# Second-mixer weights split into two parts once, kept in HBM, and loaded as two parts by every group

## What is computed

```python
# layer 0, token mixer A: gated MLP with a masked 128x128 mixing matrix per channel group
u, v, z = split(h @ w_in, 3)                       # a_w_in: 1024 x 6144
y = gelu(u) * (mix(layer_norm(gelu(v))) + b_s) * silu(z)
x = x + gate_a * (y @ w_out)                       # a_w_out: 2048 x 1024
# once: the shared keys and values
k, v = split(rms_norm(x, kv_norm) @ w_kv, 2)       # w_kv: 1024 x 256, rotary on k
# layer 1, token mixer B: sliding-window attention with sinks
q, z = split(h @ b_w_in, 2)                        # b_w_in: 1024 x 2048, rotary on q
o = softmax_with_sink(q k^T in bands of 128) @ v
x = x + gate_b * ((o * silu(z)) @ b_w_out)         # b_w_out: 1024 x 1024
return rms_norm(x, final_norm)
```

## Time and profile before

| | us |
|---|---|
| median of 3 runs | 2426.22 |
| lowest and highest of them | 2418.42 and 2426.76 |
| the profiled execution, its own time | 2430.8 |
| its span on the core | 2429.0 |
| PE busy in the span | 2274.2 |
| DVE, POOL, ACT busy | 1314.8, 1116.1, 947.8 |

### The profile page before, as it was taken

The page is one execution under the profiler, slowest core; times in us unless marked ns, Lnnn a source line. Parts: engine busy times, 40 slices in busy tenths (PEclk is TensorE's granted clock), DMA queues, the critical chain, the costliest instruction groups (busy, mean ns, idle before and its releaser), DMA issues.

```text
span 2429.0 us, 28242 instructions
## 1 busy us (share of the span) xinstructions
PE 2274.2 (94%) x10725; PEld 1899.4 (78%) x10725; DVE 1314.8 (54%) x1767; ACT 947.8 (39%) x1730; POOL 1116.1 (46%) x646
## 2 busy tenths in 40 slices
PE   3999999999999999999999999969789989998898
PEld 2787878888888888888888888857767877787786
DVE  5647891315744315644414554266577577657854
ACT  3223233433333433333423333344445545445553
POOL 3345554444444344444444443424544555564554
PEclk9999999999999999999999999989899999999999
DMA  7753334433434333344333346473634464573433
GB/s 278 268 202 114 128 130 165 165 97 120 147 113 169 128 119 117 121 144 156 121 104 105 122 140 224 134 251 102 237 106 159 176 239 132 187 256 130 156 113 113
DMA packets 188327, 375.73 MB, mean 155 GB/s; under 512 B 14272, under 2 KB 85024, under 8 KB 187552
## 3 DMA queue, kind: packets, MB, share of 16 engines
q1 hardware_dynamic: 185760, 368.65, 44.3%
q10 hardware_dynamic: 2432, 5.28, 0.6%
HBM read 295.23 MB, written 69.21 MB: 150 GB/s over the span
## 4 chain that ended last, share of the span: by engine, by line
PE 76%; DVE 10%; DMA 5%; DVEq 2%; issue 2%; ACT 2%; POOL 1%; SPq 1%; POOLq 0%; ACTq 0%
PE ps L1461 23%; PE ps L1463 23%; PE ps L1462 23%; PE ps L1611 2%; DMA w_raw<-in_a_w_out 1%; DMA r<-b_input 1%; PE ps L1649 1%; PE ps L1650 1%; POOL w_lo L704 1%; DVE wh L1305 1%; DVEq L1404 1%; DVE y_hl L1259 1%; DVE qs L1375 1%; DMA w_raw<-in_b_w_in 1%; PE ps L1673 1%
## 5 line engine op out<-in xcount | busy, mean ns | idle before, releaser
L704 POOL TENSOR_TENSOR w_lo<-w_raw,w_hi 128x1024 fp32r<-128x1024 f32 x360 | 900.9, 2513 | 991.1 <-ACT w_hi L814 990.7
L814 ACT ACTIVATE w_hi<-w_raw 128x1024 fp32r<-128x1024 f32 x360 | 380.3, 1061 | 822.6 <-DMA w_raw<-in_a_w_in 519.0
L1461 PE MATMUL ps<-h,w_hi 128*128 128x512 f32 x1024 | 402.3, 393 | 0.0
L1462 PE MATMUL ps<-h,w_hi 128*128 128x512 f32 x1024 | 398.9, 390 | 0.0
L1463 PE MATMUL ps<-h,w_lo 128*128 128x512 f32 x1024 | 398.8, 389 | 0.0
L1461 PE MATMUL ps<-r,w_hi 128*128 128x512 f32 x512 | 212.9, 416 | 26.8 <-DMA r<-b_input 11.3
L1463 PEld LDWEIGHTS ps<-h,w_lo 128*128 128x128 f32 x1024 | 192.5, 188 | 40.6
L1462 PEld LDWEIGHTS ps<-h,w_hi 128*128 128x128 f32 x1024 | 192.6, 188 | 39.5 <-issue 0.2
L1461 PEld LDWEIGHTS ps<-h,w_hi 128*128 128x128 f32 x1024 | 192.6, 188 | 39.2 <-POOL w_lo L704 0.2
L1462 PE MATMUL ps<-r,w_hi 128*128 128x512 f32 x512 | 206.1, 403 | 0.0
L1463 PE MATMUL ps<-r,w_lo 128*128 128x512 f32 x512 | 206.1, 402 | 0.0
(11 more groups left out here) (200 smaller groups left out, 4093.1 us busy)
## 6 DMA issues: line engine op xcount, KB each, us to landing
w_raw<-in_a_w_in SPq DMA_DIRECT2D x256, 256.0 KB, 3.0
w_raw<-in_a_w_in SPq DMA_DIRECT2D x64, 512.0 KB, 4.7
w_raw<-in_a_w_out SPq DMA_DIRECT2D x64, 512.0 KB, 4.1
w_raw<-in_b_w_in SPq DMA_DIRECT2D x64, 512.0 KB, 4.6
kv_input<-xks SPq DMA_DIRECT2D x32, 512.0 KB, 5.7
b_input<-hbs SPq DMA_DIRECT2D x32, 512.0 KB, 6.5
r<-b_input SPq DMA_DIRECT2D x16, 1024.0 KB, 10.9
w_raw<-b_out_gated SPq DMA_DIRECT2D x32, 512.0 KB, 4.2
```

What stands on the lines that cost most here:

```text
L704: g.tensor_tensor(wlo[p][:, rows_], raw[p][:, rows_], whi[p][:, rows_].bitcast(F32), ALU.subtract).then_inc(w_lo, 1)
L814: s_.activation(whi[p][:, rows_], raw[p][:, rows_], ACT.Copy).then_inc(w_hi, 1)
L1461: t_.matmul(dst_, stat[0], mov[0], start=start, stop=False)
L1462: t_.matmul(dst_, stat[0], mov[1], start=False, stop=False)
```

## The change

The weights of the second mixer are split once. The 26 halves (`SPLIT_UNITS`: kv, then q, z and b) are taken one for each stage of the first mixer (`LOAD_STAGES`: six in group 0, nine in each of groups 1 and 2, two in group 3). A stage is one slab j of v or one channel group g. In stage q SP loads a half into `wsr`; in stage q + 1 ACT rounds it into `wsh`, POOL subtracts into `wsl` (and multiplies by the gate first for b); in stage q + 2 SP stores both parts to `wsd` in HBM. In the second mixer each half is then loaded as two transfers, straight into `w_hi` and `w_lo`, and PE waits on the transfers. ACT's `hi` and POOL's `lo` are gone there, and so is the separate gating of b_w_out. The core of the diff:

```diff
+SPLIT_UNITS = [("kv", 0, 0)] + [(kind, n, ku) for kind in "qzb" for n in range(2) for ku in range(2)]
+SPLITS = 2 * len(SPLIT_UNITS)
+LOAD_STAGES = [(i, q) for i in range(NG) for q in range(1 if i else 4, 10)][:SPLITS]
...
+def split_at(i, q, later):
+
+    return LOAD_STAGES.index((i, q - later)) if (i, q - later) in LOAD_STAGES else None
...
-            return 16 * sum(2 if w < FIRST_B and U_UZ <= w % A_UNITS < U_AO else 1 for w in range(u % 2, u + 1, 2))
+
+            return 16 * sum(2 if w >= FIRST_B or U_UZ <= w % A_UNITS < U_AO else 1 for w in range(u % 2, u + 1, 2))
...
             def b_half(u, hh):
                 p = u % 2
-                kind, g, n, ku = B_UNITS[u - FIRST_B]
-                there = raw[p][:, 2 * hh:2 * hh + 2]
+                for m, w in ((0, whi[p]), (1, wlo[p])):
+                    sp.dma_start(w[:, 2 * hh:2 * hh + 2].bitcast(F32), wsd[split_of(u, hh), m]) \
+                        .then_inc(raw_in[2 * p + hh], 16)
+
+            def load_split(s):
+                m, (kind, n, ku), hh = s % 2, SPLIT_UNITS[s // 2], s % 2
                 kt = 4 * ku + 2 * hh
+                if s >= 2:
...
+            def keep_split(s):
+                sp.wait_ge(split_lo, s + 1)
+                sp.dma_start(wsd[s, 0], wsh[s % 2][:].bitcast(F32)).then_inc(split_out[s % 2], 16)
+                sp.dma_start(wsd[s, 1], wsl[s % 2][:].bitcast(F32)).then_inc(split_out[s % 2], 16)
+
+            def split_stage(i, q):
+                for later, act_ in ((2, keep_split), (0, load_split)):
+                    s = split_at(i, q, later)
+                    if s is not None:
+                        act_(s)
...
-                    for n in range(2):
-                        sp.wait_ge(wb_out[n], 16 * KT // 2)
+                    split_stage(i, j)
...
                         keep_turned(i - 1, g - 2)
-                    if i == 1 and g == 2:
+                    if g < GROUPS:
+                        split_stage(i, 4 + g)
...
+            def split(i, q):
+
+                s = split_at(i, q, 1)
+                if s is None:
+                    return
+                m, (kind, n, ku) = s % 2, SPLIT_UNITS[s // 2]
+                if kind == "b":
+                    pool.wait_ge(dve_pro, 4)
+                    pool.wait_ge(split_in[m], 16 * (s // 2 + 1))
+                    pool.nop(nofuse=True)
+                    g.tensor_tensor(wsr[m][:], wsr[m][:], gate_b[:, None, 512 * n:512 * n + 512].broadcast_to([P, 2, T]),
+                                    ALU.mult).then_inc(split_gated, 1)
+                pool.wait_ge(split_hi, s + 1)
+                g.tensor_tensor(wsl[m][:], wsr[m][:], wsh[m][:].bitcast(F32), ALU.subtract).then_inc(split_lo, 1)
...
                 for n in range(3, 10):
                     lo(first + n)
+                    if n % 2 == 1:
+                        split(i, (n - 3) // 2)
...
-                for u, hh in weights_at(pc):
-                    lo(u, (hh,))
...
+            def split(i, q):
+
+                s = split_at(i, q, 1)
+                if s is None:
+                    return
+                m = s % 2
+                if SPLIT_UNITS[s // 2][0] == "b":
+                    act.wait_ge(split_gated, s + 1 - 2 * SPLIT_UNITS.index(("b", 0, 0)))
+                else:
+                    act.wait_ge(split_in[m], 16 * (s // 2 + 1))
+                if s >= 2:
+                    act.wait_ge(split_out[m], 32 * (s // 2))
+                s_.activation(wsh[m][:], wsr[m][:], ACT.Copy).then_inc(split_hi, 1)
...
                     hi(first + U_UZ + 2 * g + 3)
+                    split(i, 4 + g)
...
-                for u, hh in weights_at(pc):
-                    hi(u, (hh,))
...
                 p = u % 2
                 if kt % 4 == 0:
-                    pe.wait_ge(w_lo, 2 * u + kt // 4 + 1)
+                    pe.wait_ge(raw_in[2 * p + kt // 4], landed(u))
```

More of the change, by code:

```diff
@@ L121, in order, with splits_by, split_of @@
     return (k % 4, k // 4) if by_halves(u) else (k // 2, k % 2)
[L124 to L134, removed]
+SPLIT_UNITS = [("kv", 0, 0)] + [(kind, n, ku) for kind in "qzb" for n in range(2) for ku in range(2)]
[3 more added lines that the diff above has]
+    return LOAD_STAGES.index((i, q - later)) if (i, q - later) in LOAD_STAGES else None
+def splits_by(i, m):
+    return sum(1 for s, (g, _) in enumerate(LOAD_STAGES) if g <= i and s % 2 == m)
+def split_of(u, hh):
+    kind, g, n, ku = B_UNITS[u - FIRST_B]
+    return 2 * SPLIT_UNITS.index((kind, n, ku)) + hh
 def turned_at(pc):
@@ L257, in yoco_kernel @@
         zo = [place(f"zo{n}", gb_at + 2 * K * n, [T], F32) for n in range(2)]
-        fn = place("fn", region(4 * K), [D], F32)
-        cs = place("cs", region(4 * K), [2, T], F32)
+        fn_at, cs_at = region(4 * K), region(4 * K)
+        fn = place("fn", fn_at, [D], F32)
+        cs = place("cs", cs_at, [2, T], F32)
         hfx_at, xst_at = region(4 * K), region(4 * K)
@@ L335, in yoco_kernel @@
         xr_in, xl_in = sem("xr_in", 16), sem("xl_in")
-        wb_in, wb_out = [sem(f"wb_in{n}") for n in range(2)], [sem(f"wb_out{n}") for n in range(2)]
+        split_in, split_out = [sem(f"split_in{n}") for n in range(2)], [sem(f"split_out{n}") for n in range(2)]
         sw_in = [sem(f"sw_in{n}") for n in range(2)]
@@ L359, in yoco_kernel @@
         sin_done = sem("sin_done")
-        w_lo = sem("w_lo")
+        w_lo, split_lo = sem("w_lo"), sem("split_lo")
         pool_pro, pool_mask, zeroed = sem("pool_pro"), sem("pool_mask"), sem("zeroed")
         x_rstd, v_rstd, x1_rstd, x2_rstd = sem("x_rstd", 1), sem("v_rstd", 1), sem("x1_rstd", 1), sem("x2_rstd", 4)
-        p_norm, pt_masked, wb_gated = sem("p_norm"), sem("pt_masked"), sem("wb_gated")
+        p_norm, pt_masked, split_gated = sem("p_norm"), sem("pt_masked"), sem("split_gated")
         dve_pro, ada_used = sem("dve_pro"), sem("ada_used")
@@ L439, in _ @@
             wb = b_w_in[0].rearrange("(k p) n -> p k n", p=P)
-            wbo = wbod.rearrange("k p n -> p k n")
+            wbo = b_w_out[0].rearrange("(k p) n -> p k n", p=P)
             def a_half(u, hh):
@@ L760, in _ @@
                     g.memset(kvf[:, 0, P:2 * P], 0.0).then_inc(zeroed, 1)
-                lo(first + 32)
-                lo(first + 33)
+                else:
+                    lo(first + 32)
+                    lo(first + 33)
             x1_stage(NG - 1)
@@ L849, in turned_round @@
                 act.wait_ge(t1_full, at("t1_full", i, kt + 1))
-                if i == 0 and kt == 0:
-                    act.wait_ge(wb_out[0], 16 * KT // 2)
                 if before:
@@ L884, in _ @@
                     hi(first + 2 * j + 3)
+                    split(i, j)
                 if i == 0:
@@ L1739, in b_piece @@
                 if k in ((0, 4) if by_halves(u) else (0, 1)):
-                    pe.wait_ge(w_lo, 2 * u + hh + 1)
+                    pe.wait_ge(raw_in[2 * (u % 2) + hh], landed(u))
                 if k == 0 and kind == "b":
```

49 lines of the change are left out of this document (17 added, 32 removed).

## The result

The changed kernel takes 2477.4 us (median of four runs, 2474.8 to 2481.1), the kernel before, run beside it, 2424.6: a ratio of 1.022, 95% interval 1.020 to 1.025. That is 53 us slower, and slower than the range of the prediction. In the one profiled execution that each trace shows, the difference is smaller, 2474.9 - 2429.0 = 45.9 us of span: that of the kernel before was one of its slower ones.

The account below looks back on a forecast made before the run. PE was taken to bound the first mixer, and late softmax work and transfers to idle it in the second. 34.5 + 22.6 - 36 = +21 us on 2430.8 gave 2451.9, as a median 2447; range 2412 to 2472.

Parts of the forecast that it names:

- first mixer, waits of SP: First mixer: SP's wait for `split_lo` delays the even units' weights and lowers the clock, 34.5 us, between 8 and 60.
- doubled loads: Second mixer: two transfers a half delay `r<-b_input` 16.6 us, plus clock 3 and the exchange `zo<-tt` 3, 22.6 us.
- relief: Second mixer: removed POOL and ACT work saves 24 + 3 + 3 + 6 = 36 us, between 15 and 55.
- issued some 6.5 us later than now: First mixer: subtraction 2.4 us, two stores and one load put the next even unit's load 6.5 us later.
- g = 7: Last channel group, first mixer: late AO0 weights cost 4.2, 4.2 and 7.7 us in groups 0 to 2.
- the claimed slack of 2 us: Plain u and z stages, first mixer: `w_lo` ready at 681, PE needs it at about 683.6, so it fits.
- Where v gives way to u and z: First mixer, groups 1 to 3: late `w_lo` of the even unit costs 1.2, 1.2 and 4.7 us.
- Rival 2: SP's wait stalls PE in every first-mixer stage, 25 to 30 us over the central case, 2472 us; chance 0.15.
- The clock: First mixer: four waits over 4 us lower PE's clock, 2 us each, 8 us; the second mixer's relief counts 6.
- the 45%: Second mixer: DVE's stretch during POOL's L704 makes up 8.4 of 18.5 us in three sampled waits.
- replace 8 alike: First mixer: 8 new gatings on POOL replace 8 existing ones, so no gain was counted for their removal.
- Rival 1: Relief outweighs: 39 us off value-product waits, 55 in all, SP's wait costing 12, so 2406 us; chance 0.2.

Follow-up runs that it names:

- both_off: Changed kernel with SP's split stores moved between even and odd unit's loads and the next slab's load behind the odd unit's, first mixer: 2393.6 us.
- no_gate: Kernel before the change without the gating of b_w_out in group 0, the gate left out of the computation: 2412.8 us.
- second_alone: Changed kernel with its first mixer free of gating, splits and stores; the second mixer loads other weights of the same size: 2387.0 us.
- hi_only: Changed kernel loading only the rounded part of each half in the second mixer, output not the reference's: 2456.0 us.
- keep_wait: Changed kernel with only the next slab's load, and its wait for the stores' landing, moved between even and odd unit: 2437.8 us.
- last_keep: Changed kernel with one pair of stores a group, that ahead of AO0, moved between AO0 and AO1: 2443.6 us.
- pool_back: both_off with POOL's second-mixer subtractions put back on spare data, nobody waiting for them: 2438.2 us.
- act_back: both_off with ACT's second-mixer copies put back on spare data, nobody waiting for them: 2394.6 us.

## Why the prediction was wrong

The direction was right, the size was not: 2447 forecast, 2477 measured. By the traces:

| term | forecast | measured | from |
|---|---|---|---|
| first mixer, waits of SP | +34.5 | +89 | both_off |
| gating that goes | 0 | -14 (no_gate: -8 to -13) | second_alone, no_gate |
| splits' own work | 0 | +6 | both_off less second_alone |
| doubled loads | +22.6 | +20 | hi_only |
| relief | -36 | -55 | -34.8 less the 20.4 of the loads |

The measured terms add up to the 46 us between the two traces, not to the 53 between the medians; each is a difference of single executions.

**The step that failed** is the one in "What is added in the first mixer" that has the next even unit "issued some 6.5 us later than now", with "two stores and one load" counted as if they only had to be issued. SP's wait for `split_lo` was worked out rightly: at g = 7 it was to pass at "719" in place of 713.19, 5.8 us later. Counted from the moment PE was ready for `vs`, AO0's load went out 729.47 - 713.19 = 16.3 us ahead before, and 750.21 - 740.17 = 10.0 us now: 6.3 later. What was left out is the second wait, which the code of `load_split` shows: `split_out`, the landing of stores issued two lines above. With it SP stands still for up to 5.1 us more in a stage, 58.3 us in 18 waits, and the claimed slack of 2 us is overdrawn in about half of the 26 stages: away from g = 7, PE has 13 waits of 0.65 to 4.3 us that the kernel before has not. keep_wait shows the price: 42 us for this wait alone, which the forecast had at nothing. The trace of the kernel before could have given a warning, in the row of L519 above. The wait that was forecast, for POOL, was mis-sized too: last_keep puts its part ahead of AO0 at 32 us, where the forecast had 16.1 and 6 of clock. Where v gives way to u and z, 1.2, 1.2 and 4.7 us were forecast, and PE waits 4.1, 4.3 and 3.7. Rival 2 named the symptom, every stage paying, but from another cause and at 25 to 30 us.

**g = 7** was seen as the place (PE idle 4 to 8 us was the sign to look for), and mis-sized: 4.2, 4.2 and 7.7 us more were forecast for groups 0 to 2. The waits are 10.6, 10.3 and 13.5 us where they were 3.0, 0.8 and 0.8 (only the second of these was read), so 7.6, 9.4 and 12.7 more. Four us are `vs` beside POOL's next subtraction, an overlap that I looked for at `y_rest` (5.16 us, forecast about 4.9) and not one instruction further. The Trainium skill ("SBUF — State Buffer", Who interferes with whom) lets DVE in its two-port mode and GpSimd exclude each other for a whole instruction. By that a `vs` of 0.4 us that starts behind a subtraction of 2.4 lasts until it ends; the trace agrees, with 2.44 us as its longest there, though no row says that `vs` ran in that mode.

**The clock** was counted in steps of 2 us for four waits, 8 in all. Measured are 28 us in the first mixer, and in the second the relief contains 752.8 - 737.2 = 15.6 where I had 6. With each of the waits of 10 us and more goes a stretch of 13.6 or 13.7 us at a granted clock of 0.50. It begins within the wait and ends behind it, and PE is busy in it for 5.73 and 4.62 us (changed kernel, windows):

```profile
752.60:766.20 13.60, 5.73 (x24) 5.44 (x25) 13.27 (x18) 4.30 (x7) 4.75 (x3) 0.50 0.36 137
1660.50:1674.20 13.70, 4.62 (x13) 3.77 (x14) 2.74 (x4) 0.83 (x2) 0.00 (x0) 0.50 1.03 411
```

I had taken one price, that of a wait of 5 us, and left the many waits of 2 to 4 us without one. In the first mixer of the changed kernel seven of the eleven waits of 2.2 to 4.3 us have a stretch at half speed of 3.4 or 6.8 us at their end, and four have none.

**Relief.** Waits ahead of the value product: about 25 us forecast, 22.4 measured. The size was right, and pool_back confirms POOL as the source. That it works through DVE's stretch, from which the 45% were worked out, and not through POOL's queue is not shown; that ACT "gets out from behind the weights" is worth little (act_back). The term is short by 19 us in two places. PE's idle time, 851.4 - 752.8 = 98.6 us before and 796.2 - 737.2 = 59.0 in hi_only, fell by 39.6 where I had 30, since small waits (for `tt`, `hbs`, the kv copies) went or shrank too; and the clock gave 10 more than I counted. L1448's mean was forecast at 0.5 to 0.6 us and is 0.447. No wait of the second mixer is on weights, as forecast.

**Loads.** The sum was near, 22.6 against 20.4 us, but in part by luck. The first q unit of group 0 waits 11.3 us, as worked out; those of the other groups wait 3.0, 3.6 and 4.1 us, where 8 to 11 was the sign to look for. The waits for `r<-b_input` are 21.9 us in all, and in hi_only:

```profile
PE ps L1500 <- DMA r<-b_input: 15.0, 4, 6.7
```

So the doubled loads add 6.9 us there, where 16.6 were forecast, and 1.6 us of busy time. The rest of the 20.4 lies in waits that had a smaller term or none: 4.2 us for `pp`, 2.4 for `r<-kv_input`, 2.2 ahead of the first logits (L1688), 1.8 for `r<-oz_kept`, 1.1 for `tt`. Why `pp` is later with the doubled loads is open. DMA moved 411 GB/s in the last row under "The clock". The 358 GB/s of the Trainium skill ("DMA: Bandwidth & Descriptors", Specifications) was exceeded here too, and the Trainium skill ("Perfetto Trace Analysis", Roofline) says of a core alone that it can pass that figure.

**A term of the wrong sign.** The eight gatings "replace 8 alike", so I took their removal from group 0 at nothing. POOL's work is alike; what goes with the gating is 8 to 14 us, and the likely cause is SP's waits for landings ahead of the even units (L519, 32.3 us). This would be the same mistake from the other side: both times I priced the engine's work and not the wait on the queue that issues the loads.

Rival 1 had the relief at 55 us, which is what it was, but from other parts: it took 39 us off the waits ahead of the value product, which lost 26.4. Had SP's waits been harmless, the kernel would have gained as both_off does.

## What to carry to other kernels

A queue that issues loads in order must not hold a wait whose cause is young: look for every wait between two prefetches, the landing of a store included, and count how late it makes the *next* load. Place such a wait a unit later, where it has long been met: the same work then cost 6 us in place of 95. When one wait of PE is added, price the clock by its own length, and follow the delayed chain to the engine overlap that it slides into.

## What the runs showed of the hardware

- The clock cost a third of the loss: 28.3 of 89 us, in stretches at half speed of 3.4 or 6.8 us at the end of most waits of 2 to 4 us, and of 13.7 with those of 10 and more.
- DVE's `vs`, with one tensor in SBUF as its input, stretches from 0.40 to 2.44 us beside POOL's subtraction, not only the operations with two such inputs.
- 26 slabs of 0.5 MB read, rounded, subtracted and stored as two parts cost a PE-bound stretch 6 us (two single traces) once nobody waits for them, and 13.7 us of the queue ran at 411 GB/s.
- SP waited up to 5.1 us for the landing of two stores of 0.5 MB that it had just issued. Eighteen such waits, 58.3 us in all, stood in front of loads; they cost the kernel 42 us.
